# A hybrid diffusion layer: gathered-row steps spread differently over four stages, and a shorter end of each top-16 search

## The reference, cut to what matters

```python
s = jnp.einsum('thik,hink->thin', q, sub_keys)
v_half, i_half = lax.top_k(s, TOPK)
cand = (v_half[:, :, 0, :, None] + v_half[:, :, 1, None, :]).reshape(t, PEER_HEADS, TOPK * TOPK)
top_v, top_pos = lax.top_k(cand, TOPK)
idx = jnp.take_along_axis(cand_idx, top_pos, axis=-1)
g = jax.nn.softmax(top_v, axis=-1)
u = expert_u[idx]
act = jax.nn.gelu(jnp.einsum('thkd,td->thk', u, xb))
v = expert_v[idx]
return jnp.einsum('thk,thkd->td', g * act, v)
```

## Time and profile before

| | |
|---|---|
| median of 3 runs | 2765.86 us (2756.92 to 2766.56) |
| the profiled execution | 2774.53 us, span 2772.6 us |
| PE busy | 2348.7 us (85%) |
| DVE busy | 1821.7 us (66%) |
| POOL busy | 1135.0 us (41%) |
| ACT busy | 610.0 us (22%) |
| DMA | 701.59 MB, mean 253 GB/s |

### The profile page before, as it was taken

How to read it: one execution, slowest core, us unless ns; L and a number is a source line. 1 busy time by engine, 2 the same in 40 slices (tenths; PEclk the granted TensorE clock), 3 DMA queues, 4 the chain that set the end, 5 groups by cost and what they waited for, 6 DMA issues and landing times.

```text
span 2772.6 us, 26768 instructions
## 1 busy us (share of the span) xinstructions
PE 2348.7 (85%) x8858; PEld 1470.8 (53%) x8858; DVE 1821.7 (66%) x3451; ACT 610.0 (22%) x1485; POOL 1135.0 (41%) x944
## 2 busy tenths in 40 slices
PE   6998888899999998999969999767999999999000
PEld 1354544544555544477468888665666666444000
DVE  0335767744100559887779997998666676667988
ACT  0113452522211113311222111482000001000010
POOL 0002312221000115766533234435567777576775
PEclk9889999999999999999989999888999999999555
DMA  7601111113184558999776688768999999999898
GB/s 264 227 31 31 54 38 30 64 43 116 70 277 166 186 182 305 373 375 402 271 276 203 226 303 318 278 213 325 399 395 400 389 403 363 402 395 385 306 344 296
DMA packets 236965, 701.59 MB, mean 253 GB/s; under 512 B 20912, under 2 KB 45616, under 8 KB 235568
## 3 DMA queue, kind: packets, MB, share of 16 engines
q0 software_dynamic: 112896, 411.09, 39.8%
q1 hardware_dynamic: 123232, 286.40, 28.4%
q10 hardware_dynamic: 720, 2.62, 0.2%
HBM read 686.93 MB, written 13.11 MB: 252 GB/s over the span
## 4 chain that ended last, share of the span: by engine, by line
PE 37%; DVE 19%; DMA 15%; POOL 15%; issue 9%; ACT 3%; DVEq 0%; SPq 0%; ACTq 0%; POOLq 0%
PE bank L880 11%; DMA arena<-in_peer_v,arena 8%; PE bank L1096 7%; POOL arena L1650 7%; POOL arena L1642 6%; PE bank L1054 4%; PE bank L734 4%; DVE arena L2022 3%; DMA arena<-in_peer_u,arena 2%; PE bank L775 2%; DVE arena L1808 2%; DVE arena L2000 2%; DMA arena<-in_w_ada 2%; PE bank L693 2%; POOL arena L1696 1%
## 5 line engine op out<-in xcount | busy, mean ns | idle before, releaser
L1642 POOL DMA_INDIRECT arena<-in_peer_u,arena x384 | 498.0, 1297 | 830.5 <-DVE arena L2000 471.1
L2022 DVE SCALAR_TENSOR_TENSOR arena<-arena 128x1024 f32<-128x1024 f32 x381 | 498.2, 1307 | 121.0 <-DMA arena<-in_peer_v,arena 113.2
L2000 DVE CUSTOM_DVE_ANT_0 arena<-arena 128x1024 f32<-128x1024 f32 x384 | 474.4, 1242 | 145.6 <-DMA arena<-in_peer_u,arena 141.6
L1650 POOL DMA_INDIRECT arena<-in_peer_v,arena x384 | 444.5, 1157 | 235.3 <-DVE arena L2022 121.0
L880 PE MATMUL bank<-arena 128*128 128x512 f32 (+1 forms) x1472 | 509.0, 507 | 16.1 <-DMA arena<-in_w_in 5.6
L1127 PE MATMUL bank<-arena 128*128 128x512 f32 x1024 | 453.2, 595 | 15.5 <-DMA arena<-in_peer_v 15.5
L1096 PE MATMUL bank<-arena 128*128 128x256 f32 x2048 | 452.9, 379 | 0.7 <-ACT arena L1477 0.7
L1096 PEld LDWEIGHTS bank<-arena 128*128 128x128 f32 x2048 | 389.0, 190 | 81.0 <-issue 30.6
L880 PEld LDWEIGHTS bank<-arena 128*128 128x128 f32 x1472 | 282.3, 193 | 238.5 <-issue 199.5
L1127 PEld LDWEIGHTS bank<-arena 128*128 128x128 f32 x1024 | 195.3, 191 | 235.3 <-issue 227.3
L734 PE MATMUL bank<-arena 128*128 128x512 f32 x384 | 184.0, 627 | 7.8 <-ACT arena L1191 6.5
(11 more groups left out here) (241 smaller groups left out, 2388.0 us busy)
## 6 DMA issues: line engine op xcount, KB each, us to landing
arena<-in_peer_ut SPq DMA_DIRECT2D x128, 512.0 KB
arena<-in_peer_v SPq DMA_DIRECT2D x128, 512.0 KB
arena<-in_w_in SPq DMA_DIRECT2D x22, 2048.0 KB
arena<-in_w_ada SPq DMA_DIRECT2D x12, 2048.0 KB
arena<-in_w_ssd_out SPq DMA_DIRECT2D x8, 2048.0 KB
arena<-in_w_query SPq DMA_DIRECT2D x8, 2048.0 KB
arena<-in_w_fourier SPq DMA_DIRECT2D x4, 2048.0 KB
arena<-in_w_out SPq DMA_DIRECT2D x4, 2048.0 KB
```

Source lines behind the costliest of these rows:

```text
L1642: nc.gpsimd.indirect_dma_start(rowbuf[slot], None, a["peer_u"], bass.IndirectOffsetOnAxis(ap=entries(IDX, k), axis=0)).then_inc(row_in[slo ...
L1650: nc.gpsimd.indirect_dma_start(rowbuf[slot], None, a["peer_v"], bass.IndirectOffsetOnAxis(ap=entries(IDX, k), axis=0)).then_inc(row_in[slo ...
L2000: V.tensor_tensor_reduce(out=rowbuf[slot], in0=rowbuf[slot], in1=h2c if item < PH else h2a[:, item // PH - 1, :], scale=1.0, scalar=0.0, o ...
L2022: STT(pv, rowbuf[slot], w, pv, ALU.mult, ALU.add).then_inc(s("vc_used"), 1)
```

## The change

It has five parts.

1. `WITH` has one step more for each of four tiles in seven jobs (FO1, GA0, GA1; SO2, SO3, WO0, WO1): 144 context steps lie in the tail, where there were 116. The call `context_steps(4)` behind it is gone, and `CTX_BESIDE` is left with 4 steps.
2. With the steps the context's `gates` move to other places on ACT. Those of the last group, which stood among the latents' queries, now stand at tile 1 of WO1.
3. `APART_BESIDE` has 32 steps where it had 24, and begins at head 3; `APART_EARLY` is 39 where it was 27. `START_1` goes from 51 to 71 and `START_BETWEEN` from 66 to 86. POOL's order follows, its multiplications included.
4. Searches of tiles 1 and 2 move: the first three stand behind heads 1, 4 and 6, and number 6 stands at step 70 where it stood at 82. The gates of the third group of tiles 1 and 2 go to block position 62. Those of the first and the second stay at 54 and 58.
5. The end of a search masks the 16 positions with 0xF0 and with 15 in one instruction, where it had a shift, a mask and a cast, and compares them as 32-bit numbers with places 0, 16, ..., 240 and 0, 1, ..., 15; for whole tiles the reduction writes into both index tables at once, where two copies followed it.

```diff
-WITH = {"FO1": (1, 1, 1, 1), "GA0": (1, 1, 1, 1), "GA1": (1, 1, 1, 1), "Z0": (2, 2, 2, 2), "Z1": (2, 2, 2, 2),
+WITH = {"FO1": (2, 2, 2, 2), "GA0": (2, 2, 2, 2), "GA1": (2, 2, 2, 2), "Z0": (2, 2, 2, 2), "Z1": (2, 2, 2, 2),
         "Z2": (2, 2, 2, 2), "Z3": (2, 2, 2, 2), "GB0": (3, 3, 3, 3), "SO0": (2, 2, 2, 2), "SO1": (2, 2, 2, 2),
-        "GB1": (3, 3, 3, 3), "SO2": (2, 2, 2, 2), "SO3": (2, 2, 2, 2), "WO0": (2, 2, 2, 2), "WO1": (2, 2, 2, 2)}
+        "GB1": (3, 3, 3, 3), "SO2": (3, 3, 3, 3), "SO3": (3, 3, 3, 3), "WO0": (3, 3, 3, 3), "WO1": (3, 3, 3, 3)}
-CTX_BESIDE = (5, 5, 5, 5, 4, 4, 0, 0)
-APART_BESIDE = (0, 0, 0, 0, 0, 8, 8, 8)
-APART_TOP_BESIDE = {3: 0, 5: 1, 7: 2}
-APART_TOP_AT = {16 * n - 14: n for n in range(3, 2 * PH)}
-APART_EARLY = 27
+CTX_BESIDE = (4, 0, 0, 0, 0, 0, 0, 0)
+APART_BESIDE = (0, 0, 0, 6, 6, 6, 7, 7)
+APART_TOP_BESIDE = {1: 0, 4: 1, 6: 2}
+APART_TOP_AT = {16 * n - (14 if n != 6 else 26): n for n in range(3, 2 * PH)}
+APART_EARLY = 39
...
-        if step < START_1:
+        if step + 8 < START_1:
             where = ("first", 54 + 4 * n)
...
+            for item in late:
+                gates(item)
...
-                if half == 8:
-                    for item in late:
-                        gates(item)
...
-                TS(tij[:, 0:16], tp, 4, None, ALU.logical_shift_right)
-                ch(TS(tij[:, 16:32], tp, 15, None, ALU.bitwise_and))
-                ch(CP(tijf, tij))
-                ch(TT(eq, iota16[:].unsqueeze(1).broadcast_to([P, 32, 16]), tijf.unsqueeze(2).broadcast_to([P, 32, 16]),
-                      ALU.is_equal))
+                ch(TT(tij, tp.unsqueeze(1).broadcast_to([P, 2, TOPK]), masks[:], ALU.bitwise_and))
+                ch(TT(e4, places[:].unsqueeze(2).broadcast_to([P, 2, TOPK, TOPK]),
+                      tij.unsqueeze(3).broadcast_to([P, 2, TOPK, TOPK]), ALU.is_equal))
...
-                ch(V.tensor_reduce(pick, eq, AX.X, ALU.add))
                 if t in WHOLE:
-                    for half in range(2):
-                        last = CP(ij_w[half][:, t - 3, TOPK * h:TOPK * h + TOPK], pick[:, 16 * half:16 * half + 16])
-                    last.then_inc(s("topw_done"), 1)
+                    V.tensor_reduce(ij_pair[:, :, t - 3, TOPK * h:TOPK * h + TOPK], e4, AX.X, ALU.add).then_inc(s("topw_done"), 1)
                 else:
+                    ch(V.tensor_reduce(pick, eq, AX.X, ALU.add))
...
-            context_steps(4)
             for h in range(PH):
```

More of the change, by code:

```diff
@@ L220, in gates_of_apart @@
         step = after_step(n)
-        if step < START_1:
+        if step + 8 < START_1:
             where = ("first", 54 + 4 * n)
         elif step < START_BETWEEN:
-            where = ("build", (step - START_1) * UNITS // sum(APART_BUILD))
+            where = ("build", max(0, step - START_1) * UNITS // sum(APART_BUILD))
         elif step < START_LAST:
@@ L328, in layer_kernel @@
         stat = sb("stat", [P, 64])
-        iota16 = sb("iota16", [P, TOPK], BF16)
+        places = sb("places", [P, 2, TOPK], U32)
+        masks = sb("masks", [P, 2, TOPK], U32)
         KB = 256
@@ L435, in layer_kernel @@
         ij_w = [at(kb, 2 * PICKS).rearrange("p (t n) -> p t n", t=2) for kb in (109, 139.25)]
+        apart = (139.25 - 109) * KB
+        ij_pair = at(109, 2 * int(apart)).rearrange("p (h n) -> p h n", h=2)[:, :, 0:2 * PICKS].rearrange("p h (t n) -> p h t n", t=2)
         d_w = at(140.25, 2 * PICKS).rearrange("p (t n) -> p t n", t=2)
@@ L463, in layer_kernel @@
         tv, tp = small[:, 4, 0:TOPK], small[:, 4, TOPK:].bitcast(U32)
-        tij, tijf = small[:, 5].bitcast(U32), small[:, 6, 0:TOPK].bitcast(BF16)
+        tij = small[:, 5].bitcast(U32).rearrange("p (h k) -> p h k", h=2)
         dots = [small[:, 7, 0:TOPK], small[:, 11, 0:TOPK]]
@@ L1727, in _ @@
             CP(selb[:], sel[:])
-            CP(iota16[:], shp[:, 6, 0:TOPK])
+            CP(places[:, 1, :], shp[:, 6, 0:TOPK])
+            TS(places[:, 0, :], shp[:, 6, 0:TOPK], float(TOPK), None, ALU.mult)
+            V.memset(masks[:, 0, :], TOPK * (TOPK - 1))
+            V.memset(masks[:, 1, :], TOPK - 1)
             V.memset(eps[:], EPS)
```

## The result

The changed kernel takes 2777.31 us (median of 7 runs, 2771.62 to 2786.05), the kernel before, run beside it, 2768.31 (7 runs): ratio 1.0041, 95% interval 1.0025 to 1.0057. It is slower by 0.4%, some 9 us, where 24 were forecast. A run's ratio is taken against executions of the kernel before beside it, so times of different runs are compared by their ratios. The profiled execution took 2773.75 us, span 2771.5.

A forecast was written before the change was run, and what follows sets the result against it. PE and DMA were taken as full between the v blocks, with DVE holding the build and leftover steps running alone at the end. 18 + 4 + 65 - 63 = +24 us on the median 2765.86 gave 2790 us, range 2764 to 2810.

The forecast's parts named there:

- The gate at step 40: ACT's gates stay at block position 54, so DVE's step 40 can't pass earlier relative to the queries; time spared becomes waiting.
- The build's start, +65: Twenty more steps and two more searches between step 40 and the build start it 65 us later; bounds 59 and 70.
- PE's standstill: Ahead of PE's first work in the build: idle some 75 us, where it was 11.60.
- SO2 and SO3, +18: In the DMA-full tail, seven more context steps at 2.60 us each cost 18 us before the queries.
- The tail hides its steps: Rival: row buffers and PE's lead absorb SO2 and SO3's 8 steps, queries start unchanged, about 2770 us; chance 0.18.
- WO0 and WO1, +4: Tail before the queries: changed step mix costs nothing, ACT's moved gates cost 4 us; bounds 0 and 14.
- The end of the PE-bound part, -63: Kernel's end: 20 more steps are done when PE finishes, leaving out 63 us; bounds 52 and 66.
- the lower bound of my sum: Kernel's end: 52 us saved if only the DMA time of 20 steps counts, 2.60 us each.
- the build isn't held: Rival: the 20 extra steps run in DVE's idle time ahead of position 54, giving -41, 2725 us; chance 0.1.
- The tail costs double: Rival: ACT's waits at new gate places stop PE from GA1 on, giving +45, 2811 us; chance 0.14.
- The search's end: End of each search of tiles 1 and 2: 0.3 us saved, counted only for the three behind step 40.

The follow-up runs named there:

- the early gates: Changed kernel with ACT's gates of the first two groups of tiles 1 and 2 behind block positions 42 and 50 instead of 54 and 58: 2750.86 us, ratio 0.9947.
- first pair of traces: First profiled executions of the kernel before (2774.53 us) and the changed kernel (2773.75 us), no edit in either.
- the steps alone: Kernel before with 20 steps and a search more ahead of the build, tail and search's end as before: 2759.27 us, ratio 0.9972.
- The run with two steps: Changed kernel with 2 steps after each tile of WO0 and WO1 instead of 3, eight steps moved beside whole searches: 2760.16 us, ratio 0.9987.
- second pair of traces: Both kernels run and traced again without edits: changed kernel 2780.82 us, ratio 1.0046; kernel before 2772.73 us.

## Why the prediction was right, and where its sum was off

The time lies inside the range (2764 to 2810) and on the slower side, as forecast. But +9 us is far less than +24: it falls among the outcomes within 0.5%, which had 0.19, and not among those slower by over 0.5%, which had 0.70. That it came out inside the range is owed in part to errors that cancel.

**The gate at step 40: right.** The weights came 324 us after the first queries, as before (323). DVE waited 33.78 + 10.34 us for ACT; the time freed ahead of it was lost, and the early gates got 26 to 27 us of it back.

**The build's start, +65: right.** Measured from the weights to the build: +68 in the first pair of traces (37.1 to 105.3), +65 in the second (40.1 to 105.5), and +73 with the steps alone, above the bound of 70. PE's standstill is 79.74 us (forecast 75), the build began at 1861 (forecast 1858).

**SO2 and SO3, +18: the step was right, its cover was missed.** From the first merge of SO2 to the last of SO3 it is 73.4 us where it was 50.8: 22.6 more for seven steps, 3.2 each where I had 2.60. The DMA gave 391 GB/s, not 403, which over the whole 73.4 us makes 2.2 of the 4.6 us that are missing; the rest stays open. But the position sum came only 13.3 us later. The last merge moved by 19.6 us, but SP's load of the position table stood 8.5 us behind it before, and stands 2.5 behind it now (SP in order of time, before):

```profile
1328.08 0.38 SPq L629 DMA_DIRECT2D arena<-in_pos  x1
```

and in the changed kernel:

```profile
1341.70 0.38 SPq L632 DMA_DIRECT2D arena<-in_pos  x1
```

I read this as PE having worked off what stood ahead of the last transposes while DVE was slower. The load took 14.9 and 14.6 us. "The tail hides its steps" was right for 6 of the 19.6 us. Of the page that I weighed there (the Trainium skill, "DMA: Bandwidth & Descriptors", "Where 436 GB/s comes from"): the estimate by its figure, 20.5 us for the seven steps, lies nearer to the 22.6 than mine, but its rate doesn't hold; 391 GB/s went in this stretch, and 402 in the last v blocks.

**WO0 and WO1, +4: too low.** From the position sum to the queries it is 7.8 us more (67.9 to 75.6). The run with two steps shows where: the 16 v rows alone take 1.33 us each instead of 1.2, 2 us in all, and DVE waits 4.6 us for four of them, where it waited for no row there before. The two errors cancel: the queries came 21.1 us later where 22 were forecast (26.3 in the second pair of traces).

**The end of the PE-bound part, -63: this term failed.** The step was "when PE has finished, 20 more steps are done", and its bounds were 52 and 66. There were 26.5 more in the first pair of traces and 22 in the second. Over all traces the mean is 217.0 steps with 51 ahead (four traces) and 241.1 with 71 ahead (nine): 24.1. The part behind PE's end is 196.6 us in the mean of the four and 116.2 in that of the nine: **-80**, not -63. PE ended 88.6 and 90.4 us later in the two pairs (forecast 18 + 4 + 65 = 87), and 89.5 - 80 is the +9 that was measured.

What makes the 80 of the 63: first, the count. By the first v block the changed kernel has 3.5 steps more than 67.5 + 20, and about as many at PE's end; the trace that I read was itself some 3 steps behind its siblings there, which makes the 26.5 of the first pair. Second, the price. In the rows of before, 26.5 steps went from 2569.6 to 2650, 80.4 us or 3.03 each with one search among them; at that price 24.1 are 73 us. Third, a term that the sum left out but for 3 us in its bound: the same later steps run faster in the changed kernel. From step 241 to step 255 it is 42.7 us before and 35.8 now, for the same 45 instructions of DVE (columns as in the earlier trace rows; before):

```profile
2653.20:2695.90 42.70, 0.00 (x0) 0.00 (x0) 35.22 (x45) 0.00 (x0) 34.17 (x29) 0.50 0.95 344
```

and in the changed kernel, right behind PE's end:

```profile
2659.60:2695.40 35.80, 0.00 (x0) 0.00 (x0) 35.17 (x45) 0.00 (x0) 27.19 (x26) 0.53 1.03 410
```

Over the same traces as above the means are 41.1 and 36.6 us, so this gives 4 to 5 of the 7 us that are left.

What sets the pace of the steps there stays open. POOL's groups (count, busy, mean ns, idle and its releaser), in the kernel before, 2575 to 2604:

```profile
L1642 POOL DMA_INDIRECT arena<-in_peer_u,arena x11 | 12.0, 1091 | 3.4 <-issue 3.4
L1650 POOL DMA_INDIRECT arena<-in_peer_v,arena x10 | 11.6, 1156 | 3.0 <-issue 3.0
```

and in the changed kernel, 2662 to 2696:

```profile
L1652 POOL DMA_INDIRECT arena<-in_peer_v,arena x14 | 14.9, 1065 | 5.3 <-issue 5.3
L1644 POOL DMA_INDIRECT arena<-in_peer_u,arena x11 | 12.3, 1116 | 3.4 <-issue 3.4
```

POOL waits for nobody, only 0.3 to 0.4 us between two issues: 30.0 us for 21 rows before, 1.43 a row and 2.87 a step, where the lower bound of my sum took the DMA's 2.60. Between 2604 and 2660 POOL waited for DVE once, 5.7 us in a search; 26.5 x 2.87 + 5.7 = 81.8 is close to the 80.4. But this isn't a fixed price of an issue. The 35.9 us for 25 rows in the changed kernel are a mean of unlike parts: in the first 20 us, 2662 to 2682, POOL issues 16 rows in 20.7 us, 1.29 a row, with a DMA share of 1.03 at 410 GB/s. Before, the DMA share is 0.97 at only 356 GB/s. So longer issues of POOL may hold the DMA back, or slower transfers may lengthen the issues; no run changed either, and the rows don't tell which.

**Of the rivals**, "the build isn't held" fell at its own point. "The tail costs double" fell too: ACT's gates at their new places cost nothing that shows apart from the WO part. The measured +9 is near the +6 of "the tail hides its steps", but that is luck: its tail doesn't hide the steps, and the last part makes up for it. The search's end was counted at 0.3 us for each of three searches; by itself it gives 0.26% (0.09 to 0.42), so if the gains add, the rest of the change costs more than the result shows.

## What to carry to other kernels

Where work is moved from behind a bound stretch to the front of it, count how many steps are done at its end in more than one trace before a price is put on the part left out, and price those steps from rows of the same kind; here the same steps took 2.56 us each in one kernel and 3.05 in the other. A wait that opens on a fixed place in another engine's program swallows all that is saved ahead of it: moving that place (two constants here, 26 to 27 us) was worth more than the whole change. When the waits for an engine are gone, look at the DMA share of the stretch into which the work moves: at 399 GB/s a further 10 us earlier brought nothing.

## What the runs showed of the hardware

The 128x512 compare of 32-bit numbers into bf16 takes 0.69 us, the same as the bf16 compare with a broadcast operand (693 ns). An issue of a gather of 512 KB took POOL 1.09 to 1.16 us in the mean and 0.3 us between two, 1.43 us a row, while the DMA moved 356 GB/s (before, 2575 to 2604); it took 0.94 to 1.06 us, 1.29 a row, while the DMA moved 410 GB/s (changed kernel, 2662 to 2682). The same gathers and blocks together moved at 387 to 402 GB/s in the last v blocks.
